# Sixteen of 240 gate scatter-adds on GpSimd moved from ahead of the first row gather to between the gathers

## The reference, cut to what matters

```python
q = (a @ w_q).reshape(B, S, PEER_HEADS, PEER_QDIM)          # 8 heads
...                                                          # two top-16 of 128 keys, then top-16 of the 256 pairs
gates = jax.nn.softmax(top, axis=-1)                         # 8 heads x 16 picks for each token
u_sel = jnp.take(u_exp, e_c, axis=0)                         # 16384 experts, rows of 2048
h = jnp.einsum('bthkd,btd->bthk', u_sel, a_c, preferred_element_type=jnp.float32)
w = (g_c * jax.nn.gelu(h)).astype(a_c.dtype)
v_sel = jnp.take(v_exp, e_c, axis=0)
return jnp.einsum('bthk,bthkd->btd', w, v_sel)
```

## Time and profile before

| | us |
|---|---|
| median of 3 runs | 3241.17 |
| lowest and highest of the 3 | 3237.96, 3245.41 |
| the profiled execution, its own time | 3231.75 |
| its span in the trace | 3229.9 |
| TensorE matmuls busy (97% of the span) | 3125.2 |
| VectorE busy (68%) | 2189.7 |
| GpSimd busy (40%) | 1304.1 |
| ScalarE busy (31%) | 1002.6 |

### The profile page before, as it was taken

One profiled execution on the slowest core, in us unless ns is written; L12 is line 12 of the kernel. 1 busy time (PEld: TensorE's weight loads), 2 busy tenths in 40 slices (PEclk: granted clock), 3 DMA queues, 4 the chain that ended last, 5 costly groups with the idle time before them and its releaser, 6 DMA issues.

```text
span 3229.9 us, 42906 instructions
## 1 busy us (share of the span) xinstructions
PE 3125.2 (97%) x16812; PEld 2932.2 (91%) x16812; DVE 2189.7 (68%) x3013; ACT 1002.6 (31%) x1036; POOL 1304.1 (40%) x687
## 2 busy tenths in 40 slices
PE   8999999999999995999999998999999999999998
PEld 6888678899999995999899998999999999999887
DVE  5565653566666664667666788788888888887545
ACT  5234432332233331222222232323323222233422
POOL 1010000028888888878787323333333233330000
PEclk9999999999999997999999999999999999999999
DMA  8472213245555555999999889888888888885322
GB/s 304 142 251 92 79 66 104 92 135 135 134 129 130 130 135 160 331 307 333 300 323 325 352 342 355 319 311 331 311 312 315 315 328 308 319 310 194 104 102 91
DMA packets 209414, 739.19 MB, mean 229 GB/s; under 512 B 71953, under 2 KB 125201, under 8 KB 132993
## 3 DMA queue, kind: packets, MB, share of 16 engines
q1 hardware_dynamic: 90768, 409.55, 34.9%
q0 software_dynamic: 100080, 302.69, 29.1%
q10 hardware_dynamic: 18432, 25.17, 2.2%
HBM read 682.60 MB, written 54.72 MB: 228 GB/s over the span
## 4 chain that ended last, share of the span: by engine, by line
PE 63%; POOL 27%; issue 5%; DMA 2%; DVE 2%; ACT 0%; SPq 0%; DVEq 0%; ACTq 0%; POOLq 0%
POOL gates L442 23%; PE ps L1489 20%; PE ps L1490 20%; PE ps L1491 20%; POOL rows_u L459 4%; DMA gates<-gates_r,idx_d 1%; PE ps L1662 1%; PE ps L1681 1%; PE ps L1661 0%; DVE wL L819 0%; DMA raw<-s_v 0%; DMA rows_v<-u_rows,idx_s 0%; DVE ssum L831 0%; DMA rows_u<-u_rows,idx_s 0%; DVE hT L1458 0%
## 5 line engine op out<-in xcount | busy, mean ns | idle before, releaser
L1489 PE MATMUL ps<-aH,wH 128*128 128x384 f32 (+2 forms) x3088 | 1091.5, 353 | 61.9 <-DVE wL L819 59.8
L1490 PE MATMUL ps<-aL,wH 128*128 128x384 f32 (+2 forms) x3088 | 1085.6, 352 | 0.0
L1491 PE MATMUL ps<-aH,wL 128*128 128x384 f32 (+2 forms) x3088 | 1085.5, 352 | 0.0
L476 ACT ACTIVATE wH<-raw 128x2048 fp32r<-128x2048 f32 x333 | 637.9, 1916 | 1050.7 <-PE ps L1491 976.7
L442 POOL DMA_INDIRECT gates<-gates_r,idx_d x384 | 758.0, 1974 | 397.8 <-DVE gates_r L1211 255.5
L819 DVE TENSOR_TENSOR wL<-raw,wH 128x2048 fp32r<-128x2048 f32 x333 | 761.7, 2287 | 230.2 <-ACT wH L476 229.0
L1489 PE MATMUL ps<-actH,wH 128*128 128x384 f32 x2048 | 685.3, 335 | 9.0 <-DVE wL L819 6.3
L1490 PE MATMUL ps<-actL,wH 128*128 128x384 f32 x2048 | 684.8, 334 | 0.0
L1491 PE MATMUL ps<-actH,wL 128*128 128x384 f32 x2048 | 684.8, 334 | 0.0
L1489 PEld LDWEIGHTS ps<-aH,wH 128*128 128x128 f32 x3088 | 582.5, 189 | 107.3 <-DVE wL L819 66.0
L1490 PEld LDWEIGHTS ps<-aL,wH 128*128 128x128 f32 x3088 | 582.7, 189 | 38.4 <-issue 1.0
(11 more groups left out here) (244 smaller groups left out, 1812.3 us busy)
## 6 DMA issues: line engine op xcount, KB each, us to landing
raw<-s_pu SPq DMA_DIRECT2D x128, 1024.0 KB
raw<-s_pv SPq DMA_DIRECT2D x128, 1024.0 KB
gates<-zeros POOLq DMA_DIRECT2D x24, 1024.0 KB, 8.6
pre<-ut ACTq DMA_DIRECT2D x128, 192.0 KB
pre_in<-pre SPq DMA_DIRECT2D x128, 192.0 KB
gate_in<-gates SPq DMA_DIRECT2D x128, 192.0 KB
raw<-s_out SPq DMA_DIRECT2D x16, 1024.0 KB
raw<-s_pq SPq DMA_DIRECT2D x16, 1024.0 KB
```

The costliest lines, as they stand in the source:

```text
L476: A(wH[parity][:, :], raw[parity][:, :], ACT.Copy).then_inc(hi_ready, 1)
L1489: mm(out, wh, xh, start=start, stop=False)
L1490: mm(out, wh, xl, start=False, stop=False)
L1491: return mm(out, wl, xh, start=False, stop=stop)
```

## The change

The constant of 5 heads becomes a count of 224 adds. So 224 instead of 240 adds stand ahead of the wait for `a_tok_ready` and the first gather. The loop behind it is the same and deals out what is left: 160 adds instead of 144, five for three gathers. 144 adds are used up behind gather 85, 160 behind gather 95. The adds, their order among themselves, their waits, and all other engines' programs are the same.

```diff
-HEADS_FIRST = 5
+ADDS_FIRST = 224
...
-            added = HEADS_FIRST * NTD * TOPK
+            added = ADDS_FIRST
             for n in range(added):
                 add_gates(n)
```

## The result

The changed kernel takes 3215.14 us (median of 4 runs, 3206.14 to 3218.87) against 3239.57 us (4 runs, 3237.95 to 3245.41). The ratio is 0.9917, with a 95% interval of 0.9892 to 0.9942. That is 24.4 us less, where 24.0 was forecast, and 3215.1 where 3217.2 was. A second set of runs gave 3212.82 against 3237.50, ratio 0.9919 (0.989 to 0.9947).

What follows compares the result with a forecast made beforehand. GpSimd's backlog of adds was taken to delay gather 0, stopping VectorE and TensorE, and to bound the interleaved stretch. -27.3 + 1.9 + 1.4 = -24.0 us, from 3241.17 to 3217.2 us; range 3210.5 to 3229.5.

Steps and rivals of the forecast that it cites:

- Gather 0 comes earlier: GpSimd's first gather starts at 1220.9 instead of 1248.23 us, then held only by `a_tok`: 27.3 us gained.
- TensorE's wait falls to about 5.6 us: TensorE's longest wait, for the low part of its weights near gather 0, falls from 32.85 us, by 27.3.
- Sixteen adds in the stretch give back 1.9 us: Interleaved stretch: three more rounds bound by GpSimd, 17.28 us each where TensorE would take 16.64, cost 1.9 us.
- Three waits move: First adds of heads 5, 6 and 7 wait for the head before at other places: 14.7 us, 1.4 more.
- SyncE's wait and the clock count nothing: SyncE's wait for all adds keeps a 39 us margin; TensorE's 1.2 GHz restart may shorten; both counted as nothing.
- Sum of TensorE's waits: TensorE's waits between 1180 and 2100 us fall from 65.2 to near 41 us.
- Rounds clearly over 17.7 us: Sign of being wrong: rounds of three gathers and five adds in the interleaved stretch taking clearly more than 17.7 us.
- Rival 1: Moved adds in the interleaved stretch cost nothing, so nothing of the 27.3 us is given back: 3213.9 us, chance 0.12.
- Rival 2: GpSimd's stall is moved, not removed; the gain is lost in small waits later: 3235 to 3241 us, chance 0.09.
- Rival 3: The last add lands too late for SyncE's wait, stopping the weights: slower, some 3248 us, chance 0.05.
- The lower end of the range: 3210.5 us for the whole kernel: rival 1, waits at their lower bound, about 3 us scatter of the median.

Runs made afterwards that it cites:

- first pair: Profiled executions of the kernel before and the changed kernel, from the first measurement: 3231.75 and 3218.87 us.
- second pair: No edit: the kernel before and the changed kernel each profiled once more, 3237.16 and 3210.58 us in the profiled executions.

## Why the prediction was right, point by point

The profiled spans, cut at three gathers, against the forecast (changes in us):

| stretch | forecast | first pair | second pair |
|---|---|---|---|
| up to gather 0 | -27.3 | -30.1 | -28.5 |
| gather 0 to 84 | the waits, +1.4 | +10.8 | -6.3 |
| gather 84 to 117 | +1.9 | +2.9 | +4.4 |
| behind gather 117 | 0 | +3.6 | +3.8 |
| whole | -24.0 | -12.9 | -26.6 |

- **Gather 0 comes earlier, by 27.3 us, and `a_tok` is late next: right.** The rows show 30.1 and, in the second pair of traces, 28.5 us; `a_tok` released it both times. The step counted on `a_tok` at 1220.6, and in the first trace of the changed kernel it was there at 1217.8, by what one execution differs from another and not by the change (in the traces with 224 or 208 ahead gather 0 starts at 1218.1 to 1222.7). Alone, this step is worth 24.7 us in the medians of the two kernels without later adds.
- **TensorE's wait falls to about 5.6 us: right,** 5.99 measured.
- **Sixteen adds in the stretch give back 1.9 us: right in mechanism, small in size.** GpSimd is the bound up to gather 95, and its first wait for VectorE is at gather 98 and not 89, at 1799.86 less 3.61, near the 1795 forecast. The part where the two kernels have different work, behind gather 84, takes 2.9 and 4.4 us more. What moves the whole by more than that is the stretch ahead of it, where the work is the same but for the places of the waits.
- **Three waits move, 1.4 us more: right in place, and small.** Head 5's add waits 6.72 us behind its predecessor (6.3 forecast). The three together take 12.9 us against 13.3, so 0.4 less and not 1.4 more: behind a gather they cost 3.95 and 2.23 where 4.2 each was taken.
- **SyncE's wait and the clock count nothing: right.** SyncE has no wait for adds in the changed kernel's trace. The forecast allowed that the slow restart might be shorter behind a short gap; it is not, the clock is 0.50 in the four microseconds behind both, so it adds nothing to the difference.
- **Sum of TensorE's waits, 41 us forecast:** 46.9 and 40.9 in the two traces. Without the longest one they rose by 8.5 and 3.2 us, where 3.3 was forecast.
- **Behind gather 117 the forecast has nothing,** and both pairs show 3.6 to 3.8 us more. Over all traces of this document this part takes 1291.5 to 1297.8 us, and the two of the kernel before are among the three shortest. Whether it is the change or chance stays open.
- **Rounds clearly over 17.7 us were named as a sign of being wrong.** The first trace shows 18.07 and the second 17.58, so the sign was one that a single execution can't give.
- **Rival 1, the moved adds cost nothing because VectorE does not lengthen them: wrong in its reason, and not excluded by its time.** Its 3213.9 lies as near to the medians 3215.14 and 3212.82 as the forecast's 3217.2. Against it stands the count of adds above, which shows that VectorE does lengthen them. The forecast left open whether the longer adds came from the traffic. They don't. The Trainium skill ("SBUF — State Buffer", "Who interferes with whom") has, beside the sentence on `tensor_tensor` and DMAs that the forecast took, another one: a VectorE instruction with two inputs in SBUF contends with a GpSimd instruction that reads SBUF, and one with at most one such input, outside the two-port modes, does not. The counts agree with the second: 44 of 44 and 57 of 57 held with two inputs in SBUF, none of 40 with one of them in PSUM. They do not agree with a `tensor_tensor` that leaves DMAs alone: `lo` is such an instruction, and 30 long adds before end 1.41 to 1.46 us behind it. What an indirect DMA on GpSimd reads from SBUF while it is held, no run shows.
- **Rival 2, the stall is moved and not removed: excluded** by the medians.
- **Rival 3, the deadline of SyncE: its place was shown** with 208 ahead, its price at 224 is nothing.
- **The lower end of the range does not follow from its terms.** Rival 1's 3213.9 with the waits at their lower bound (4.0 us less than before) and 3 us of scatter gives 3206.9, and 3210.5 was written. The measured median lies above both.

That the sum came within 0.4 us is partly luck. The first step is 24.7 us in the medians where 27.3 was taken, and the whole is 24.4, so what was given back is near nothing there, where 3.3 was taken: two errors of some 3 us that cancel, each no larger than what the medians tell apart. What the forecast did not see is that the profiled execution is one draw: it took 17.28 us of work in a round as a constant. From the profiled execution it had 3207.8, and the two profiled executions of the changed kernel took 3218.87 and 3210.58. The medians carried the forecast; judged by the first pair of profiles alone it would have looked half wrong.

## What to carry to other kernels

An engine at 40% of the span can hold the end in one stretch: follow its longest wait to the queue behind it, and ask which wait comes last once that is gone; here the gain ended at `a_tok`, and moving 16 adds more lost 6 to 8 us. Work that is only deferred into a stretch where its engine is the bound has to be priced there, and may be dealt out as thinly as its deadline allows. Where GpSimd issues many small DMAs beside VectorE, look whether the long ones end at a fixed distance behind VectorE instructions with two inputs in SBUF; putting one input into PSUM gave 34 to 36 us, more than the move of the adds.

## What the runs showed of the hardware that was not expected

- An indirect DMA on GpSimd of 1.55 us takes up to 3.6 us when it starts while a VectorE instruction with two fp32 inputs in SBUF runs (`scalar_tensor_tensor` or `tensor_tensor`, 128 x 2048, 2.28 us), and then ends 1.41 to 1.46 us behind it. Started up to 0.02 us behind the start of such an instruction it is not held; started 0.1 to 1.9 us behind, it always was (101 of 101 beside dots in the first two traces). With one of the inputs in PSUM it takes 1.54 to 1.58, at the same length of the VectorE instruction.
- With half dots and with one input in PSUM many rounds are TensorE's 16.64 us exactly, one behind the other, while GpSimd hardly waits for VectorE. In the traces of the kernels before and after, single rounds up to gather 84 take 15.4 to 23.6 us. The same program had a mean of 17.58 in one execution and 18.07 in another. That GpSimd and VectorE falling in and out of step makes this difference is argued, not shown.
